# A decoder block on one core: the scale sums of w_mod, from double tile 2 on, done by ScalarE and one reduction on VectorE

## The reference, cut to what matters

```
mod = c @ w_mod + b_mod                        # c: 2048, w_mod: 2048 x 6144, float32
shift, scale, gate = split(mod, 3)
u = x * (1 + scale) + shift                    # x: 512 x 2048
proj = u @ w_in                                # w_in: 2048 x 12288
q, k, v, z_a, cb, cc, cx, z_b, g_a, g_b = split(proj)
...                                            # attention of 8 heads, short convolution
h = sigmoid(g_a) * (y_a @ w_proj_a) + sigmoid(g_b) * (y_b @ w_proj_b)
out = layernorm(alpha * x + gate * (h @ w_out))
```

## Time and profile before

| what | value |
|---|---|
| median of 3 runs | 1504.12 us (1501.89 to 1504.17) |
| profiled execution | 1502.2 us, its span 1500.5 us |
| TensorE busy | 1477.4 us, 98% |
| VectorE, ScalarE, GpSimd busy | 58%, 34%, 3% |
| chain that ended last | PE 97%, DVE 1%, SyncE's queue 1%, DMA 1% |

### The profile page before, as it was taken

The page is one execution under the profiler, slowest core; times in us unless marked ns, Lnnn a source line. Parts: engine busy times, 40 slices in busy tenths (PEclk is TensorE's granted clock), DMA queues, the critical chain, the costliest instruction groups (busy, mean ns, idle before and its releaser), DMA issues.

```text
span 1500.5 us, 18355 instructions
## 1 busy us (share of the span) xinstructions
PE 1477.4 (98%) x6592; PEld 1210.0 (81%) x6592; DVE 864.6 (58%) x1190; ACT 511.9 (34%) x724; POOL 48.5 (3%) x91
## 2 busy tenths in 40 slices
PE   6999999999999999999999999999999999999996
PEld 5888888878888788887888878888788888888885
DVE  7987877567565675656746568333432323444447
ACT  2334654253442534425344253232122221421120
POOL 0000000000000000000000000100000000000000
PEclk9999999999999999999999999999999999999999
DMA  9999543443544425444254442542223232363222
GB/s 355 392 330 318 189 117 116 137 136 90 161 120 136 137 86 154 130 133 140 84 152 134 133 141 78 188 150 91 84 88 108 92 103 85 110 252 112 84 84 112
DMA packets 211974, 219.18 MB, mean 146 GB/s; under 512 B 8417, under 2 KB 160353, under 8 KB 211169
## 3 DMA queue, kind: packets, MB, share of 16 engines
q1 hardware_dynamic: 200736, 176.72, 36.1%
q0 software_dynamic: 10096, 35.66, 7.8%
q10 hardware_dynamic: 1106, 6.32, 1.0%
HBM read 211.33 MB, written 7.34 MB: 146 GB/s over the span
## 4 chain that ended last, share of the span: by engine, by line
PE 97%; DVE 1%; SPq 1%; DMA 1%; issue 0%; ACT 0%; DVEq 0%
PE acc L1336 30%; PE acc L1338 30%; PE acc L1337 30%; PE sc L1468 1%; PE misc L1491 1%; PE sc L1336 1%; PE sc L1338 1%; PE sc L1337 1%; PE sc L1482 1%; DMA raw<-in_w_in 1%; SPq L388 0%; DVE mod_sum L840 0%; PE misc L1474 0%; PE misc L1338 0%; PE misc L1336 0%; PE misc L1337 0%
## 5 line engine op out<-in xcount | busy, mean ns | idle before, releaser
L1336 PE MATMUL acc<-act_hi,w_hi 128*128 128x512 f32 x1472 | 577.9, 393 | 2.7 <-DVE act_lo L887 2.7
L1338 PE MATMUL acc<-act_hi,w_lo 128*128 128x512 f32 x1472 | 573.8, 390 | 0.0
L1337 PE MATMUL acc<-act_lo,w_hi 128*128 128x512 f32 x1472 | 573.7, 390 | 0.0
L524 ACT ACTIVATE w_hi<-raw 128x1024 fp32r<-128x1024 f32 (+2 forms) x258 | 268.2, 1047 | 745.1 <-PE acc L1338 572.7
L813 DVE TENSOR_TENSOR w_lo<-raw,w_hi 128x1024 fp32r<-128x1024 f32 x254 | 306.5, 1215 | 370.0 <-ACT w_hi L524 369.5
L1336 PEld LDWEIGHTS acc<-act_hi,w_hi 128*128 128x128 f32 x1472 | 276.9, 188 | 64.4 <-DVE w_lo L813 4.4
L1338 PEld LDWEIGHTS acc<-act_hi,w_lo 128*128 128x128 f32 x1472 | 276.7, 188 | 58.2
L1337 PEld LDWEIGHTS acc<-act_lo,w_hi 128*128 128x128 f32 x1472 | 276.9, 188 | 56.9 <-issue 0.2
L1069 DVE SCALAR_TENSOR_TENSOR bias_acc<-bias_w,mod,bias_acc 128x512 f32<-128x512 f32 x48 | 36.0, 751 | 124.5 <-DMA bias_w<-in_w_in 124.5
L1336 PE MATMUL acc<-y_hi,w_hi 128*128 128x512 f32 x256 | 99.7, 389 | 0.0
L1338 PE MATMUL acc<-y_hi,w_lo 128*128 128x512 f32 x256 | 99.6, 389 | 0.0
(11 more groups left out here) (182 smaller groups left out, 1090.4 us busy)
## 6 DMA issues: line engine op xcount, KB each, us to landing
raw<-in_w_in SPq DMA_DIRECT2D x258, 256.0 KB, 6.3
raw<-in_w_tail SPq DMA_DIRECT2D x32, 1024.0 KB
raw<-in_w_in SPq DMA_DIRECT2D x25, 1024.0 KB
w_mod_in<-in_w_mod SPq DMA_DIRECT2D x32, 512.0 KB, 8.7
w_mod_in<-in_w_mod SPq DMA_DIRECT2D x16, 1024.0 KB, 7.7
gate_in<-in_w_mod POOLq DMA_DIRECT2D x32, 512.0 KB, 4.1
bias_w<-in_w_in POOLq DMA_DIRECT2D x48, 256.0 KB, 3.3
res<-in_x ACTq DMA_DIRECT2D x1, 4096.0 KB, 14.8
```

The lines of the kernel that those rows point to most:

```text
L524: return act.activation(dst, src, ACT.Copy)
L1336: pe.matmul(dst, a_hi, b_hi, start=first, stop=False)
L1337: pe.matmul(dst, a_hi, b_lo, start=False, stop=False)
L1338: return pe.matmul(dst, a_lo, b_hi, start=False, stop=last)
```

## The change

From double tile 2 on (k tile 4), ScalarE multiplies the four rows of each chunk by their elements of c in place, in `w_mod_in` (`scale_rows`, 16 instructions of 128x256 for a double tile), and VectorE adds eight rows in one TENSOR_REDUCE, twice for a double tile (`add_rows`), and then joins the two. Double tile 0 and 1 and the shift sums stay as they were. ScalarE does the rows of double tile g + 1 behind `act_hi` of g and before the `w_hi` of the next two halves; for g + 1 from 5 on, the first chunk's four rows stand ahead of the columns of g. VectorE's round is now: columns of g, `w_lo` of half 2g, `act_lo` of g, `w_lo` of 2g + 1, the two reductions of g + 1 and the join. SyncE loads all four chunks of double tile 2 before its x and weights; a chunk's slot is counted free when the reduction that read it is done. TensorE does one of the three tiles of the odd half g - 1 ahead of the `reduce_sums` of g, for g = 2, 3 and 4. The first k tile's two weight loads have a semaphore each.

```diff
+JOINT = 2
+def steps_before(q):
+    if q <= JOINT:
+        return q * MOD_CHUNKS * MOD_STEPS
+    joint = 2 * (min(q, GROUPS) - JOINT)
+    return JOINT * MOD_CHUNKS * MOD_STEPS + joint + max(q - GROUPS, 0) * MOD_CHUNKS * MOD_STEPS
...
+            def free_scale(c):
+                g, n = divmod(c, MOD_CHUNKS)
+                sp.wait_ge(mod_step, steps_before(g) + (MOD_STEPS * (n + 1) if g < JOINT else n // 2 + 1))
...
             pair_unit(1)
-            for g in range(2, GROUPS):
+            for n in range(MOD_CHUNKS):
+                scale_chunk(2 * MOD_CHUNKS + n)
+            x_pair(2)
+            pair_unit(2)
+            for g in range(3, GROUPS):
...
+            def scale_rows(g, n):
+                c = MOD_CHUNKS * g + n
+                act.wait_ge(scale_landed[c % SCALE_SLOTS], 16 * (c // SCALE_SLOTS + 1))
+                for a in range(MOD_STEPS):
+                    row = scale_in(c)[:, a, :]
+                    e = MOD_STEPS * n + a
+                    ins = act.activation(row, row, ACT.Identity, scale=c_col[:, e:e + 1])
+                ins.then_inc(scaled, 1)
...
             for g in range(1, GROUPS):
+                if 4 <= g < GROUPS - 1:
+                    scale_rows(g + 1, 0)
                 act.wait_ge(mod_ready, g + 2)
                 act.wait_ge(x_landed[g], 16)
                 for k in (2 * g, 2 * g + 1):
                     scaled_hi(k)
+                if g < GROUPS - 1:
+                    for n in range(1 if g >= 4 else 0, MOD_CHUNKS):
+                        scale_rows(g + 1, n)
                 for f in (2 * g + 2, 2 * g + 3):
                     round_at(f, 0, 0, 0)
...
+            def add_rows(g):
+                for half in range(2):
+                    first = (MOD_CHUNKS * g + 2 * half) % SCALE_SLOTS * MOD_STEPS * G_COLS
+                    rows = w_mod_in[:, first:first + 2 * MOD_STEPS * G_COLS].rearrange("p (k c) -> p c k", c=G_COLS)
+                    dve.wait_ge(scaled, MOD_CHUNKS * (g - JOINT) + 2 * (half + 1))
+                    if half == 0:
+                        dve.wait_ge(mod_reduced, g - 1)
+                    dve.tensor_reduce(mod_sum[:, g % 2, half, 0:G_COLS], rows, AX.X, ALU.add).then_inc(mod_step, 1)
+                join_sums(g)
...
-            for g in range(2, GROUPS - 1):
-                scale_sums(g + 1, 0)
+            for g in range(1, GROUPS):
                 pair_columns(g)
-                scale_sums(g + 1, 1)
+                lo_half(2 * g, 0, 0, 0)
                 scaled_lo(g)
-                lo_half(2 * g + 2, 0, 0, 0)
-                scale_sums(g + 1, 2)
-                lo_half(2 * g + 3, 0, 0, 0)
-                scale_sums(g + 1, 3)
+                lo_half(2 * g + 1, 0, 0, 0)
+                if g < GROUPS - 1:
+                    add_rows(g + 1)
...
             for g in range(1, GROUPS):
+                before = 1 if 2 <= g <= 4 else 0
+                if before:
+                    gate_half(g - 1, range(before))
                 reduce_sums(g, 2, misc[:, 2 * g:2 * g + 2])
```

More of the change, by code:

```diff
@@ L231, in decoder_block @@
         first_x = sem("first_x")
-        first_raw = sem("first_raw")
+        first_raw = [sem(f"first_raw{n}") for n in range(2)]
         first_hi = sem("first_hi")
@@ L237, in decoder_block @@
         sums_ready = sem("sums_ready")
+        scaled = sem("scaled")
         x_landed = [sem(f"x_landed{g}") for g in range(GROUPS)]
@@ L375, in first_tile @@
                 row = w_in[k * P:(k + 1) * P, GATE_A:GATE_A + (4 + G_TILES) * P]
-                landed, each = (raw_landed[0], 32) if k else (first_raw, 16)
-                sp.dma_start(raw[:, 0, k, :], row[:, 0:COLS]).then_inc(landed, each)
-                sp.dma_start(raw[:, 0, 2 + k, 0:G_TILES * P], row[:, COLS:COLS + G_TILES * P]).then_inc(landed, each)
+                for n, (c0, c1) in enumerate(((0, COLS), (COLS, (4 + G_TILES) * P))):
+                    sp.dma_start(raw[:, 0, 2 * n + k, 0:c1 - c0], row[:, c0:c1]
+                                 ).then_inc(raw_landed[0] if k else first_raw[n], 32 if k else 16)
+            def free_scale(c):
+                g, n = divmod(c, MOD_CHUNKS)
+                sp.wait_ge(mod_step, steps_before(g) + (MOD_STEPS * (n + 1) if g < JOINT else n // 2 + 1))
             def scale_chunk(c):
@@ L383, in scale_chunk @@
                 if c >= SCALE_SLOTS:
-                    sp.wait_ge(mod_step, MOD_STEPS * (c - SCALE_SLOTS + 1))
+                    free_scale(c - SCALE_SLOTS)
                 if SCALE_SLOTS <= c < SCALE_SLOTS + MOD_CHUNKS:
@@ L582, in _ @@
                     else:
-                        act.wait_ge(first_raw, 32)
+                        act.wait_ge(first_raw[f], 16)
                     copy(w_hi[:, f, k, 0:width], raw[:, 0, 2 * f + k, 0:width]).then_inc(hi_ready if k else first_hi, 1)
@@ L830, in sum_chunk @@
                 for a in range(MOD_STEPS):
-                    e = MOD_STEPS * (MOD_CHUNKS * q + n) + a
+                    e = steps_before(q) + MOD_STEPS * n + a
                     dst = mod_sum[:, q % 2, a % sums, 0:width]
@@ L852, in scale_sums, with join_sums @@
                 if n == MOD_CHUNKS - 1:
-                    dve.wait_ge(mod_step, MOD_STEPS * MOD_CHUNKS * (g + 1))
-                    both = mod_sum[:, g % 2, 0, 0:G_COLS], mod_sum[:, g % 2, 1, 0:G_COLS]
-                    dve.tensor_tensor(both[0], both[0], both[1], ALU.add).then_inc(sums_ready, 1)
+                    join_sums(g)
+            def join_sums(g):
+                dve.wait_ge(mod_step, steps_before(g + 1))
+                both = mod_sum[:, g % 2, 0, 0:G_COLS], mod_sum[:, g % 2, 1, 0:G_COLS]
+                dve.tensor_tensor(both[0], both[0], both[1], ALU.add).then_inc(sums_ready, 1)
+            def add_rows(g):
[6 more added lines that the diff above has]
+                    dve.tensor_reduce(mod_sum[:, g % 2, half, 0:G_COLS], rows, AX.X, ALU.add).then_inc(mod_step, 1)
+                join_sums(g)
             def shift_sums(d):
@@ L862, in shift_sums @@
                 if n == MOD_CHUNKS - 1:
-                    dve.wait_ge(mod_step, MOD_STEPS * MOD_CHUNKS * (GROUPS + j + 1))
+                    dve.wait_ge(mod_step, steps_before(GROUPS + j + 1))
                     dve.sem_inc(sums_ready, 1)
@@ L1361, in half, with gate_half @@
                         ins.then_inc(bank_full[n], 1)
-            def gate_half(g):
+            def gate_half(g, tiles=range(G_TILES)):
                 f = 2 * g + 1
                 pe.wait_ge(lo_ready, f + 1 + RAW_START)
-                for n in range(G_TILES):
+                for n in tiles:
                     cols = slice(n * P, (n + 1) * P)
@@ L1372, in gate_half @@
                                     act_hi[:, k, :], act_lo[:, k, :], k == 0, k == KT - 1)
-                ins.then_inc(half_done, 1)
+                if n == G_TILES - 1:
+                    ins.then_inc(half_done, 1)
             for events in (v_turned, o_done, p_turned, scores_done, half_done):
@@ L1425, in _ @@
                 else:
-                    gate_half(g - 1)
+                    gate_half(g - 1, range(before, G_TILES))
                 pe.wait_ge(u_lo_ready, 2 * g + 2)
```

18 lines of the change are left out of this document (3 added, 15 removed).

## The result

The changed kernel takes 1522.8 us (median of 4 runs, 1520.62 to 1523.66) and the kernel before 1503.84 us (1501.89 to 1504.17, 4 runs): 1.0129 times as long, 95% interval [1.0117, 1.0141]. That is 19 us more; the forecast of 1510 us meant about 6. The profiled execution took 1520.62 us, 18.4 more than that of before.

What follows compares the result with a forecast made beforehand. TensorE, 98% busy, was taken as the bound, with VectorE's shift sums setting the pace near 155 us. 1502.2 + 4.9 (later third sum) + 2.5 (lost clock) = 1509.6, given as 1510; own range 1505 to 1516, stretched to 1503 to 1531.

Steps and rivals of the forecast that it cites:

- the price of the reduction: VectorE's reduction of 2048 elements takes 2.29 us, by the slope of L1107's rows.
- The upper end of 2.75: VectorE's reduction at most 2.75 us, four times the 512 row; that would add 2.3 us to the time.
- the first rival: VectorE's reduction reads slower, 4.43 us at twice the element price; VectorE sets the pace, 1529.6 us; chance 0.22.
- 88.20: Columns' matmul of double tile 7 on TensorE forecast at 88.20 us, against 89.92 before.
- ScalarE's row: One 128x256 row multiply on ScalarE takes 505 ns, spaced 0.405 us; sixteen rows take 6.58 us.
- The order of `w_lo`: VectorE makes half 15's w_lo a round later, so gate_unit(0) leaves SyncE 4.9 us later, as do landing and third sum.
- the third sum: Third shift sum ends on VectorE at 160.0; TensorE waits about 4 us and restarts at 160.2, +4.9.
- The clock term: TensorE's wait of about 4 us before the third shift sum loses its higher clock, costing 2.5 us more.
- The wait at the second sum: Second shift sum comes at 138.7, where TensorE arrives at 136.1 and waits 2.6 us.
- No change: Rival: the DMA queue's hole closes, third shift sum stays near 155.15, time 1502 to 1505 us; chance 0.12.
- faster: Rival: TensorE's lead goes through to the end, about 5 us, time 1498 us; chance 0.05.
- The hole in the DMA queue: Gap from SyncE's later issues; the no-change rival (chance 0.12) has it close by itself.

Runs made afterwards that it cites:

- e9: Changed kernel with SyncE's order alone altered (shift chunk 0 issued before L442's unit, shift chunk 2 before gate_unit(0)): 1519.93 us, ratio 1.0116.
- e3: Kernel before with only VectorE's new order (the w_lo places), sums by multiply and add as before: 1511.44 us, ratio 1.0056.
- e1: Changed kernel with each reduction reading its 2048 elements in sequence, so its sums are wrong: 1510.25 us, ratio 1.0046 to the kernel before.
- e4: Separate program without the block's computation, timing reductions and copies at several steps: reduction 2286 ns at 2 elements, 3776 ns at 4.
- e2: Changed kernel with each reduction replaced by three additions of whole row blocks read in sequence: 1511.3 us, ratio 1.0052 to the kernel before.
- e5: e2 plus two orders: SyncE's shift chunks 0 and 2 earlier, VectorE's shift sums 4 and 5 before half 20's w_lo: 1502.24 us, ratio 0.9996.
- e10: Changed kernel with VectorE's list alone altered (shift sums 4 and 5 before the w_lo of half 20): 1516.65 us, ratio 1.0097.

## Why the prediction was wrong

**The step that failed is the price of the reduction**, 2.29 us: "both hold if a read with a step of 1024 bytes costs what one in sequence does, which no row shows". It doesn't hold: the reduction measured 3.82, and read in sequence 2.28. The upper end of 2.75 rested on the same assumption. Both values came from a row whose elements lie side by side. At 3.82 the first rival holds: its round was twice the reduction plus fixed parts, 14.7 and 13.3 for 4.43; with 3.82 that is 13.5 and 12.1, and the trace has 13.5 for the rounds of 3 and 4 and 12.1 to 12.3 for those behind. The measured 1522.8 us lies above my own range (1505 to 1516); it lies in 1503 to 1531 only because this rival had stretched that. I had given it 0.22 because I took its price as twice or nothing; it decided from 2.5 on, and the bench shows no price between 2.29 and 3.57 at any step tried.

From the forecast's 88.20 to the measured 101.52 at double tile 7 there are 13.3 us: 2.6 at double tile 2 (of them 0.6 already there at 24.80 for 24.20, which is chance: the same code starts there at 23.86 in e9), 4.2 in the rounds of 3 and 4 (26.97 for 22.80), 2.3 in that of 5 (12.07 for 9.78) and 4.3 in those of 6 and 7 (24.36 for 20.06).

**ScalarE's row**, 0.405 apart and 505 ns, was right: 499 ns, and 16 of them in 6.52 us (6.58).

**The order of `w_lo`** was right in its mechanism, and nearly so in size. Half 15 ends 104.70 + 0.95 - 101.52 = 4.13 us behind the columns (4.04), `gate_unit(0)` leaves at once, and the landing is 29.80 us later (29.74 before), the third sum 38.23 us after that (38.23 before). That this step alone makes the kernel slower, while TensorE is ahead, is e3. With the reduction at its forecast price (e1) the third sum comes at 161.71 where 160.2 was forecast.

**The clock term** of 2.5 us is not in the changed kernel: the rest behind the third sum is 1345.2 us, as before. The wait there is 0.64 us; the one of 1.68 and the clock it lost lie before it, under VectorE's pace. In e1 and e3, where the reduction's price is out of the way, the wait is 3.9 us (4 forecast) and the rest 2.6 to 2.7 longer (2.5 forecast). The wait at the second sum was 1.6 there (2.6 forecast) behind one of 1.4 for a `w_lo` (e1: 1.39 at 132.99), which the prediction had missed.

**No change and faster** fell. The hole in the DMA queue did not close: after and before have the same 29.8 us from issue to landing.

What stays open: in the kernel the reduction takes 3.82 us, in e4 3.59 at the same step. ScalarE writes the same buffer meanwhile in the kernel and nothing else ran in e4. The first reduction of each pair, with ScalarE's rows beside all of it, takes 3.89 to 3.92 us and the second 3.67 to 3.87, which fits that reason; it was not tried by itself. Nor was the changed kernel run with the split semaphore or TensorE's tile ahead taken out. For the semaphore, e3, without it, starts double tile 1 at 25.12 as e1 does at 25.02, so it shows no price; the tile ahead comes later, and nothing here prices it.

## What to carry to other kernels

A price taken from a row holds for that row's access pattern; where the new instruction reads with another step and no row has it, the upper end must come from another kind of row or a bench, not from a multiple of the same one. Before an instruction that frees a buffer is moved later, look up which issue waits for it and what stands behind that in the queue: here 6 us at one issue went undiminished to the end of the kernel (e3), although the engine that bounds it was ahead. And where an engine's list has a long wait for data, put in front of it what is ready already (for one line moved, 6 us at the third sum here and 4 at the end).

## What was not expected of the hardware

The edge between 8 and 16 bytes is not the reduction's alone. In e4 a copy of 128x2048 fp32 on VectorE takes 1227 ns at a step of 1 and of 2 elements and 2005 to 2012 at 4, whether the step is on the side read or the side written; at 16 elements it is 1898 to 1908, at 64 2299 and more. ScalarE's takes 1909 ns at 1, 2120 at 2 and 3829 at 4, and 3642 at 256. So a step of 16 bytes or more costs both engines 1.5 to 2 times, and ScalarE pays a tenth more at 8 bytes already.

TensorE's clock: a single wait of 1.63 us (at 51.65 in after) left the granted clock at 1.00 in 50 to 60 us, as did the waits of 1.1 us in each round of e2 and e5; the wait of 1.68 us at 152.37, 7.4 us behind another of 0.97, was followed by the lower level (0.66 in 150 to 160 us). But in e1 one of 1.64 us at 140.38, 7.4 us behind another of 1.39, left 1.00 in 140 to 150, and in e9 and e10 waits of 3.87 and of 1.42 us cost the same 1.6 us beyond themselves. So the length of a wait alone doesn't say here whether the clock falls, nor what that costs: behind the waits of 3.8 and 3.9 us it was 1.6 (e9) to 2.7 us (e1).
